# A whole-tile root in the norms, the modulated full value on another engine, and one conversion call fewer

## The reference

```python
def rms_norm(x, g):
    y = xf * lax.rsqrt(jnp.mean(xf * xf, axis=-1, keepdims=True) + EPS)
    return (y * g).astype(x.dtype)

h = modulate(rms_norm(x, norm_g[i, 0]), shift[:, 0], scale[:, 0])   # h * (1 + scale) + shift
x = x + MACARON_WEIGHT * gate[:, 0, None, :] * swiglu(h, ...)       # then a mixer, then a swiglu again
```

## Time and profile before

| | |
|---|---|
| median of 3 runs | 2369.22 us (2365.1 to 2369.62) |
| the profiled execution | 2364.49 us, span 2363.2 us |
| mean granted TensorE clock over the span | 0.991 |
| share of the span busy: TensorE, VectorE, ScalarE, GpSimd | 96%, 56%, 49%, 2% |
| weight bytes and others moved | 439.75 MB, mean 186 GB/s |

### The profile page before, as it was taken

How to read it: one execution, slowest core, us unless ns; L and a number is a source line. 1 busy time by engine, 2 the same in 40 slices (tenths; PEclk the granted TensorE clock), 3 DMA queues, 4 the chain that set the end, 5 groups by cost and what they waited for, 6 DMA issues and landing times.

```text
span 2363.2 us, 38278 instructions
## 1 busy us (share of the span) xinstructions
PE 2260.6 (96%) x16752; PEld 2060.3 (87%) x16752; DVE 1327.0 (56%) x1763; ACT 1155.3 (49%) x1348; POOL 57.2 (2%) x72
## 2 busy tenths in 40 slices
PE   6999998999999999899899999999999999999998
PEld 3999866999999987677699997899999988989998
DVE  2543565544455466657555445556786555667873
ACT  3443565543444354544554335654555456436553
POOL 2000000000000000000000011000000020000000
PEclk9999999999999999999999999999999999999999
DMA  8767562666575756345165555433655363445550
GB/s 311 236 229 289 196 250 68 218 223 231 187 252 196 266 192 247 128 150 205 56 214 183 192 196 175 161 125 125 211 182 191 126 233 132 154 143 179 179 196 19
DMA packets 273590, 439.75 MB, mean 186 GB/s; under 512 B 10656, under 2 KB 147152, under 8 KB 273296
## 3 DMA queue, kind: packets, MB, share of 16 engines
q1 hardware_dynamic: 270880, 429.07, 52.6%
q0 software_dynamic: 2256, 7.12, 0.9%
q10 hardware_dynamic: 288, 1.11, 0.1%
HBM read 436.22 MB, written 1.05 MB: 185 GB/s over the span
## 4 chain that ended last, share of the span: by engine, by line
PE 89%; ACT 5%; DVE 3%; DMA 1%; issue 1%; SPq 0%; POOL 0%; ACTq 0%; POOLq 0%; DVEq 0%
PE ps L1265 86%; ACT whi L1487 1%; DVE wlo L1674 1%; PE ps L1418 1%; ACT PT L1487 1%; PE ps L1365 1%; PE ps L1453 1%; DMA raw<-in_mod_w 1%; ACT xhi L1487 1%; PE ps L1428 1%; ACT L1487 1%; ACT S L1487 0%; DMA raw<-in_fox_w_in 0%; SPq L1254 0%; ACT x L1487 0%
## 5 line engine op out<-in xcount | busy, mean ns | idle before, releaser
L1674 DVE TENSOR_TENSOR wlo<-raw,whi 128x2048 fp32r<-128x2048 f32 x339 | 769.0, 2275 | 584.8 <-ACT whi L1487 584.6
L1487 ACT ACTIVATE whi<-raw 128x2048 fp32r<-128x2048 f32 x339 | 640.7, 1895 | 422.4 <-PE ps L1265 387.1
L1265 PE MATMUL ps<-xhi,whi 128*128 128x256 f32 x2888 | 733.5, 286 | 14.8 <-ACT xhi L1487 11.4
L1265 PE MATMUL ps<-xhi,wlo 128*128 128x256 f32 x2888 | 727.9, 284 | 0.0
L1265 PEld LDWEIGHTS ps<-xhi,whi 128*128 128x128 f32 x2888 | 555.7, 192 | 29.1 <-issue 27.6
L1265 PEld LDWEIGHTS ps<-xhi,wlo 128*128 128x128 f32 x2888 | 555.8, 192 | 0.3
L1265 PE MATMUL ps<-xlo,whi 128*128 128x256 f32 x2888 | 471.0, 284 | 3.6 <-DVE xlo L1892 3.4
L1265 PEld LDWEIGHTS ps<-xlo,whi 128*128 128x128 f32 x2888 | 401.4, 192 | 4.3 <-DVE xlo L1892 3.8
L1265 PE MATMUL ps<-hhi,whi 128*128 128x256 f32 x1056 | 299.0, 283 | 0.9 <-DVE modc L1687 0.9
L1265 PE MATMUL ps<-hlo,whi 128*128 128x256 f32 x1056 | 298.5, 283 | 0.0
L1265 PE MATMUL ps<-hhi,wlo 128*128 128x256 f32 x1056 | 297.5, 282 | 0.0
(11 more groups left out here) (222 smaller groups left out, 1999.6 us busy)
## 6 DMA issues: line engine op xcount, KB each, us to landing
raw<-in_mod_w SPq DMA_DIRECT2D x72, 1024.0 KB, 9.2
raw<-in_w_in SPq DMA_DIRECT2D x52, 1024.0 KB, 4.9
raw<-in_ffn_w_gate SPq DMA_DIRECT2D x88, 512.0 KB, 6.5
raw<-in_ffn_w_up SPq DMA_DIRECT2D x88, 512.0 KB, 7.8
raw<-in_ffn_w_down SPq DMA_DIRECT2D x44, 1024.0 KB, 6.7
raw<-in_w_up SPq DMA_DIRECT2D x88, 512.0 KB, 4.7
raw<-in_dil_w_in SPq DMA_DIRECT2D x36, 1024.0 KB, 5.9
raw<-in_w_down SPq DMA_DIRECT2D x22, 1024.0 KB, 4.8
```

The lines of the kernel that those rows point to most:

```text
L1265: return nc.tensor.matmul(o, lhs, rhs, start=start, stop=stop, skip_group_check=True)
L1487: return nc.scalar.activation(o, i, func, **kw)
L1674: V.tensor_tensor(wlo[:, s["c"], 0:s["n"]], raw[:, s["slot"], 0:s["n"]], whi[:, s["c"], 0:s["n"]].bitcast(F32), ALU.subtract).then_inc(sem ...
```

## The change

Four things. (1) `rstd`: ScalarE takes the root of the whole 128x256 statistic out of PSUM into `sqb` slot 0, VectorE the reciprocal of the whole in place; the diagonal product, the sum, and the two row products on TensorE are gone, and the scaling reads SBUF in place of PSUM. (2) `norm`: the full modulated value is computed by GpSimd from the scaled chunk into `sqb` slots 1 to 3; ScalarE makes the high part alone, and the low part is formed from GpSimd's value. Layer norms keep both passes on ScalarE. (3) `Tail.step` no longer calls `ensure()`. (4) The waits that guard the buffers follow.

```diff
@@ rstd, norm
-    def rstd(self, stat, eps, src=G0, dst=G1, between=None):
-        diag = self.ev("dve", "diag")
-        summed = self.ev("dve", "diag")
-        sq = self.ev("act", "sqrt")
-        rec = self.ev("dve", "recip")
+    def rstd(self, stat, eps, src=G0):
+        root = self.ev("act", "root")
+        rows = self.ev("dve", "rows")
...
-            self.nb_free[m % 4] = lo
+            self.nb_free[m % 4] = [st["x_hi"], st["x_mod"]]
+            self.sq_free[1 + m % 3] = lo
+            self.shift_read[3 * s] = lo
...
-                          shift=am, scale=bm, x_read=self.x_read, x_hi=self.ev("act", "x_hi"), x_mod=self.ev("act", "x_hi"))
+                          shift=am, scale=bm, x_read=self.x_read, x_hi=self.ev("act", "x_hi"), x_mod=self.ev("pool", "x_mod"))
@@ Tail.step
         self.more(chunks)
-        if not self.started and self.plan.in_stage:
-            self.plan.ensure()
-        self.started = True
         self.flush(self.lag)
@@ TensorE's program
-                elif k == "rows":
-                    for t in range(2):
-                        ins = mm(ps[:, s["bank"], t * P:(t + 1) * P], st[:, 2 + t:3 + t].to_broadcast([P, P]), ident[:, :],
-                                 t == 0, True)
@@ ScalarE's program
-                    q.wait_ge(s["summed"])
-                    act(st[:, 0:2], st[:, 4:6], ACT.Sqrt, bias=epst[:, s["eps"]:s["eps"] + 1]).then_inc(sem["sqrt"])
+                    q.wait_ge(s["stat"])
+                    act(rstd, ps[:, s["src"], 0:T], ACT.Sqrt, bias=epst[:, s["eps"]:s["eps"] + 1]).then_inc(sem["root"])
...
-                    act(n[:, b, :], n[:, b, :], ACT.Identity, scale=sc, bias=bi).then_inc(sem["x_hi"])
@@ VectorE's program
-                    V.reciprocal(st[:, 2:4], st[:, 0:2]).then_inc(sem["recip"])
+                    q.wait_ge(s["root"])
+                    V.reciprocal(rstd, rstd).then_inc(sem["rows"])
...
-                    V.tensor_tensor(nbufs[s["buf"]][:, m % 4, :], x[:, m, :], ps[:, G1, 0:T], ALU.mult).then_inc(sem["scaled"])
+                    V.tensor_tensor(nbufs[s["buf"]][:, m % 4, :], x[:, m, :], rstd, ALU.mult).then_inc(sem["scaled"])
...
-                    V.tensor_tensor(xlo[:, m, :], nbufs[s["buf"]][:, m % 4, :], xhi[:, m, :].bitcast(F32),
+                    V.tensor_tensor(xlo[:, m, :], sqb[:, 1 + m % 3, :], xhi[:, m, :].bitcast(F32),
@@ GpSimd's program
+                elif k == "norm":
+                    q.wait_ge(s["scaled"])
+                    q.wait_ge(s["shift"])
+                    q.wait_ge(s["scale"])
+                    q.wait_ge(s["sq_free"])
+                    c0 = 3 * s["s"] * NC
+                    V.tensor_scalar(sqb[:, 1 + m % 3, :], n[:, b, :], ascale[:, s["s"], m:m + 1], mod[:, c0 + m:c0 + m + 1], ALU.mult,
+                                    ALU.add).then_inc(sem["x_mod"])
```

More of the change, by code:

```diff
@@ L30 @@
     "const_set", "c_silu", "w_hi", "w_lo", "piece", "mod_mm", "mod_row", "mod_turned", "mod_col",
-    "square", "stat", "diag", "sqrt", "recip", "rows", "scaled", "x_hi", "x_mod", "x_lo", "resid",
+    "square", "stat", "root", "rows", "scaled", "x_hi", "x_mod", "x_lo", "resid",
     "half", "gate_act", "hidden", "h_hi", "h_lo", "score", "biased", "expd", "weighed",
@@ L67, in __init__ @@
         self.sq_free = [None] * 4
-        self.nb_free = [None] * 4
+        self.nb_free = [[]] * 4
         self.in_stage = False
@@ L252, in stat, with norm @@
         return tok
-    def rstd(self, stat, eps, src=G0, dst=G1, between=None):
-        diag = self.ev("dve", "diag")
-        summed = self.ev("dve", "diag")
-        sq = self.ev("act", "sqrt")
-        rec = self.ev("dve", "recip")
-        self.add("rstd", stat=stat, eps=eps, src=src, diag=diag, summed=summed, sqrt=sq)
-        self.free[src] = diag
-        self.sq_free[0] = summed
+    def rstd(self, stat, eps, src=G0):
+        root = self.ev("act", "root")
+        rows = self.ev("dve", "rows")
+        self.add("rstd", stat=stat, eps=eps, src=src, root=root)
+        self.free[src] = root
+        return rows
+    def norm(self, i, s, buf, stat, between=None):
+        rows = self.rstd(stat, 0)
         if between:
             between()
[L264 to L269, removed]
         if (i, s) == (0, 0):
@@ L285, in norm @@
             t1 = self.ev("dve", "scaled")
-            st = self.add("norm", m=m, s=s, buf=buf, rows=rows, nb_free=self.nb_free[m % 4], x=self.x_ready[m], scaled=t1,
-                          shift=am, scale=bm, x_read=self.x_read, x_hi=self.ev("act", "x_hi"), x_mod=self.ev("act", "x_hi"))
+            st = self.add("norm", m=m, s=s, buf=buf, rows=rows, sq_free=self.sq_free[1 + m % 3], nb_free=self.nb_free[m % 4], x=self.x_ready[m], scaled=t1,
+                          shift=am, scale=bm, x_read=self.x_read, x_hi=self.ev("act", "x_hi"), x_mod=self.ev("pool", "x_mod"))
             pend.append((m, st))
@@ L291, in norm @@
         low(*pend.pop(0))
-        self.free[G1] = t1
-        self.shift_read[3 * s] = st["x_mod"]
+        self.sq_free[0] = t1
         self.ensure()
@@ L676, in layer_norm @@
         self.free[G0] = self.x_ready[-1]
-        rows = self.rstd(tk, 1, G1, G0)
+        rows = self.rstd(tk, 1, G1)
         self.pair = 0
@@ L699, in layer_norm @@
             low(*pend.pop(0))
-        self.free[G0] = t1
+        self.sq_free[0] = t1
         self.ensure()
@@ L1225, in build @@
         rel = ret_pt
+        rstd = sqb[:, 0, :]
         ple = e1[:, :, :].rearrange("p a n -> p (a n)")
@@ L1725, in dve_program @@
                     q.wait_ge(s["rows"])
-                    q.wait_ge(s["nb_free"])
+                    for t in s["nb_free"]:
+                        q.wait_ge(t)
                     q.wait_ge(s["x"])
-                    V.tensor_tensor(nbufs[s["buf"]][:, m % 4, :], x[:, m, :], ps[:, G1, 0:T], ALU.mult).then_inc(sem["scaled"])
+                    V.tensor_tensor(nbufs[s["buf"]][:, m % 4, :], x[:, m, :], rstd, ALU.mult).then_inc(sem["scaled"])
                 elif k == "norm_lo":
                     m = s["m"]
+                    q.wait_ge(s["x_hi"])
                     q.wait_ge(s["x_mod"])
-                    V.tensor_tensor(xlo[:, m, :], nbufs[s["buf"]][:, m % 4, :], xhi[:, m, :].bitcast(F32),
+                    V.tensor_tensor(xlo[:, m, :], sqb[:, 1 + m % 3, :], xhi[:, m, :].bitcast(F32),
                                     ALU.subtract).then_inc(sem["x_lo"])
@@ L1742, in dve_program @@
                     q.wait_ge(s["x"])
-                    V.tensor_tensor(x[:, m, :], x[:, m, :], ps[:, G0, 0:T], ALU.mult).then_inc(sem["scaled"])
+                    V.tensor_tensor(x[:, m, :], x[:, m, :], rstd, ALU.mult).then_inc(sem["scaled"])
                 elif k == "ln_lo":
@@ L1960, in pool_program @@
                         q.wait_ge(t)
+                elif k == "norm":
+                    m, b, n = s["m"], s["m"] % 4, nbufs[s["buf"]]
+                    q.wait_ge(s["scaled"])
[5 more added lines that the diff above has]
+                                    ALU.add).then_inc(sem["x_mod"])
                 elif k == "rope_angles":
```

15 lines of the change are left out of this document (1 added, 14 removed).

## The result

The changed kernel takes 2383.19 us (median of 6 runs, 2380.34 to 2391.86) against 2369.95 us for the kernel before (6 runs, 2365.1 to 2371.33): the ratio is 1.0074, 95% interval 1.0058 to 1.009, so by the ratio, which this text uses throughout, it is slower by 17.5 us (13.7 to 21.3). The ratio is not that of the two medians, which lie 13.2 us apart. The forecast was 2391 us, range 2376 to 2408, or 21 us above the kernel before. The profiled execution took 2387.93 us, at a mean granted clock of 0.980; the profiled execution before stood at 0.991.

What follows compares the result with a forecast made beforehand. TensorE, busy 96% of the span, was taken as the bound, so other engines matter only where it waits, around the ten norms. Terms -1.7 - 4.5 + 20.4 + 3.5 + 2.0 + 2.8 gave +22.5 us: 2391 us, range 2376 to 2408.

Steps and rivals of the forecast that it cites:

- The head: Ten norms, last statistic to first scaled chunk: whole-tile root and reciprocal replace the small ones and their products; -1.7 us.
- rival 3: The 128x256 reciprocal is cheap, 0.42 us and not 1.69: 2380 us; chance 7%.
- The tail: Last updates behind three down projections: without the weight conversion each tail is 1.5 us shorter; -4.5 us.
- The turning up: Norm bodies: the removed conversion runs ahead of chunk 4, so TensorE waits for chunk 3's low part in eight norms; +20.4 us.
- The piece behind: Norms: the next weight piece or split of p behind the moved conversion comes late too; +3.5 us.
- The split tail: End of the first block: updates start sooner, but the next conversion is the second piece, with half a unit still following; +2.0 us.
- GpSimd: Norm chunks: the full value on GpSimd, about 0.90 us each, stays hidden under TensorE's 1.45 us; 0 us.
- Rival 2: GpSimd sets the norms' chunk pace, from 1.45 us on: 2399 us, or 2416 with a 1.5 us operation; chance 17%.
- The clock: Modulated norms: new waits of 2.4 us drop TensorE to 1.2 GHz behind six in ten of them; +2.8 us.
- Rival 1: The moved conversion stays hidden because TensorE has work in hand: 2365 us; chance 8%.
- rival 4: TensorE's new waits replace the clock loss and the tail's waits to within 0.2%: 2369 us; chance 6%.

Runs made afterwards that it cites:

- the halves in the body: The changed kernel with VectorE's half of the body's weight conversion moved behind the low part of chunk 3: 2374.36 us, ratio 1.0037.
- the first experiment: The changed kernel with the call of ensure() in Tail.step put back, so the conversion stays in the tails: 2365.38 us, ratio 0.9999.
- the filled kernel: The changed kernel with matmuls without purpose in the norms' heads and 6 before the wait for chunk 3's low part: 2386.64 us, ratio 1.0082.

## Why the prediction was right, point by point

- **Where the loss is.** Right, and shown from both sides: with the call back in the tails the ratio is 0.9999, with the call alone removed 1.0119. That about half of it is made by the place in VectorE's queue is shown by the halves in the body (1.0037).
- **The head, -1.7 us.** Measured -0.6. The price of the reciprocal was right to 0.06 us (1.75 for 1.69), which ends rival 3. The modulated norms gained 0.10 instead of 0.23: from the root's start to the first scaled chunk it takes 2.40 us (425.76 to 428.16) and not 2.26, of which the reciprocal has 0.06, the root 0.02 and longer hand-overs the rest. One modulated norm even lost 0.25: there 0.48 us pass between root and reciprocal, in the other modulated norms 0.13. In four runs (the first experiment among them) the same delay is in the norm ahead of the dilated mixer, in three others in no norm; its cause is open.
- **The tail, -4.5 us.** Measured -4.45.
- **The turning up, +20.4 us.** The mechanism is as described, with the low part of chunk 3 at 9.32 us in layer norms (9.3) and 8.4 to 8.6 in modulated norms (8.8). There the step was mis-sized: TensorE waited 1.9 us and not 2.4 in four of them, because the low part came 0.2 to 0.4 us sooner than 8.8, the 0.1 added for GpSimd never came, and in two of them TensorE wanted it 6.7 to 6.8 us behind the scaled chunk and not 6.5. In the fifth the clock had fallen ahead of the wait. By the starts of the same product in both traces each of the five norms is 2.1 to 2.2 us late once it has the low part, so the term is about 1 us too high in all. In the layer norms 2.8 was right, as the filled kernel shows.
- **The piece behind, +3.5 us.** By the starts of the same product 1.6 us between the layers (1.6), and 0.54 for the split of p in each of the two others (0.45). Behind it stands a wait that the forecast doesn't have, for ScalarE's `e`: 1.1 and 0.5 us more than before. The dilated norm's 1.0 is a wait of 0.62 us in the filled kernel; in the changed kernel slow clock covers it, as was forecast.
- **The split tail, +2.0 us.** By the starts of the same products it costs 1.9 us (its stage is 4.02 us late once the next unit runs, of which the norm ahead made 2.12). The way is the one forecast: the conversion stands at the second piece, and half a unit of products still follows.
- **GpSimd, 0.** Right with the conversion in the tails: no difference to ScalarE. Rival 2 needed 1.45 us per chunk and the pace was 1.04. The two engines do hinder each other, and GpSimd pays for most of it: its operation takes 0.55 us with nothing on VectorE beside it, and 0.81 or 0.92 in most of the others. VectorE lost time in 11 of 48 scalings (0.62 us for 0.42) and in one low part (0.70 for 0.42); with the full value on ScalarE no scaling took more than 0.47. The one low part, with the GpSimd operation that it met:

```profile
429.49 0.56 POOL L1947 TENSOR_SCALAR sqb<-nbuf,ascale,modc 128x256 f32<-128x256 f32 x1
...
429.61 0.70 DVE L1711 TENSOR_TENSOR xlo<-sqb,xhi 128x256 fp32r<-128x256 f32 x1 [0.70 <-POOL sqb L1947]
```

  The Trainium skill (SBUF — State Buffer, "Who interferes with whom") has the later instruction blocked for the whole of the other. For this low part that would be the 0.44 us that GpSimd still ran, an estimate from the rows; it lost 0.28, and most low parts that began behind a GpSimd operation's start lost nothing. So the trace shows a shorter block, and mostly on GpSimd.
- **The clock, +2.8 us.** In the profiled execution the clock fell behind two of the four waits of 1.9 us (0.68 over 3.4 us at 436.8), near the six in ten of the forecast, and the modulated stages cost 17.9 us there but 13.0 in the filled kernel. In all three layer norms it fell at the start and was swallowed by the wait, as forecast. Yet the filled kernel's time is no better (1.0082 against 1.0074). So in the timed runs the size of this term is not shown.
- **The sum.** +22.5 us was forecast between profiled executions, and 23.4 was measured there; that it fits so well is luck. The 23.4 hold the -3.0 of the start and a profile after with more slow clock than one before (0.980 against 0.991). The profile of before lies 5.5 us under the median of its runs, that of after 4.7 us above its own, and in the runs time goes with the granted clock: in the changed kernel 2387.93 and 2391.86 us at 0.980 and 0.981, 2380.34 and 2380.39 at 0.988. By the ratio the loss is 17.5 us. The filled kernel, with little slow clock at the norms, checks the body's terms best: its stages cost 13.0 and 13.3 us more than before, 26.3 together, where the forecast without the clock has 20.4 + 3.5 + 2.0 = 25.9. Within that the modulated stages were put too high and the layer norms' too low by about 2 us each.
- **The rivals.** Rival 1 (the conversion stays hidden) fell with the 1.88 us wait, rival 4 (little changes, within 0.2%) with the ratio.

## What to carry to other kernels

Before a piece of background work is removed from a place where it costs 1.5 us, find the next call that will do it and read what is queued behind it on each engine: here it moved from the end of a stage to a place between an engine and the operand it waits for, and three tails' gain of 4.5 us turned into a loss of 17.5. If such work must stand in a hot stretch, cut it at the hand-over between its engines (half of the loss came back here), and look at which barrier counts its last event. And price it with the stages' own rows: the one norm that already did what the others would do gave the 9.3 us at once.

## What the runs showed of the hardware

- The reciprocal on VectorE took 1.75 us for 128x256 (all ten), 0.253 for 128x16 and 0.163 for 128x1, where a subtraction of 128x256 takes 0.42: close to 6.2 ns for each further element, by these three rows.
- TensorE's idle time of 3.54 us in front of a layer norm was followed by stretches at 1.2 GHz in all three of the changed kernel (granted clock 0.57 over 7 us in the first) and in two of the three with the conversion in the tails (0.66 over 5 us in the last), but not in the first of those, where the clock stayed at 1.00. With matmuls without purpose in the heads and 0.86 us left idle, the last one ran at 1.00, and the kernel's ratio went from 0.9999 (0.9986 to 1.0013) to 0.9974 (0.9961 to 0.9986).
- A slower clock can be free: in the changed kernel's layer norms it filled a wait of 2.8 us to within 0.2 us, and the stages cost the same when it was raised.
- GpSimd and VectorE slow each other, and here GpSimd lost more: 0.81 or 0.92 us for an operation that takes 0.55 alone, while VectorE's took 0.42 in most cases and 0.62 in 11 scalings of 48.
